# Holding back the second layer's first weight loads until the gathers of expert rows have landed

## What is computed

```python
c_act = jax.nn.silu(c)
for l in range(DEPTH):
    mod = jnp.einsum('bd,dn->bn', c_act, w_ada[l]) + b_ada[l]
    sh1, sc1, gt1, sh2, sc2, gt2 = jnp.split(mod[:, None, :], 6, axis=-1)
    h = rmsnorm(x, g_norm1[l]) * (1.0 + sc1) + sh1
    x = x + gt1 * hybrid_mixer(h, w_in[l], ...)
    h = rmsnorm(x, g_norm2[l]) * (1.0 + sc2) + sh2
    x = x + gt2 * grouped_moe(h, w_router, b_router, w_gate[l], w_up[l], w_down[l])
return rmsnorm(x, g_final)
```

## Time and profile before

| | us |
|---|---|
| median of three runs | 1037.66 |
| lowest, highest | 1033.07, 1038.24 |
| the profiled execution's own time | 1034.82 |
| its span in the profile | 1033.0 |
| PE busy in the span | 980.5 |
| DVE busy | 585.8 |
| ACT busy | 313.7 |
| POOL busy | 88.2 |

### The profile page before, as it was taken

The page is one execution under the profiler, slowest core; times in us unless marked ns, Lnnn a source line. Parts: engine busy times, 40 slices in busy tenths (PEclk is TensorE's granted clock), DMA queues, the critical chain, the costliest instruction groups (busy, mean ns, idle before and its releaser), DMA issues.

```text
span 1033.0 us, 13163 instructions
## 1 busy us (share of the span) xinstructions
PE 980.5 (95%) x4871; PEld 613.3 (59%) x4871; DVE 585.8 (57%) x1350; ACT 313.7 (30%) x781; POOL 88.2 (9%) x83
## 2 busy tenths in 40 slices
PE   3899999999999899999989999999999998999996
PEld 1344465689745557666654445568885556577672
DVE  1359897867656643223185689796763346322327
ACT  3131323656421221112142122436662121211213
POOL 3001003000000010000140010300000000100012
PEclk9899999999999999999989999999999998999998
DMA  9986526600375699999937371140006128999946
GB/s 355 366 278 239 183 72 215 245 2 1 124 279 149 260 338 406 420 418 358 317 128 293 143 265 62 44 163 2 1 2 244 41 111 340 403 410 419 417 145 239
DMA packets 86183, 229.72 MB, mean 222 GB/s; under 512 B 35796, under 2 KB 50628, under 8 KB 71628
## 3 DMA queue, kind: packets, MB, share of 16 engines
q1 hardware_dynamic: 77192, 196.38, 50.6%
q0 software_dynamic: 5760, 20.97, 5.6%
q10 hardware_dynamic: 3168, 11.54, 2.7%
HBM read 210.99 MB, written 22.56 MB: 226 GB/s over the span
## 4 chain that ended last, share of the span: by engine, by line
PE 88%; DVE 4%; DMA 3%; ACT 2%; issue 1%; SPq 1%; POOL 0%; DVEq 0%; ACTq 0%; POOLq 0%
PE bank L1274 80%; PE bank L1291 5%; PE bank L1582 2%; DMA wbuf<-in_w_ada 2%; ACT shared L554 1%; DMA y_rows<-tok 1%; DVE x L1227 1%; DMA shared<-y_rows,ints 1%; SPq L1773 1%; DVE x L1236 0%; POOL shared L518 0%; DVE tok L1000 0%; ACT L644 0%; PE bank L1623 0%; DVE pring L1243 0%
## 5 line engine op out<-in xcount | busy, mean ns | idle before, releaser
L1274 PE MATMUL bank<-shared,wbuf 128*128 128x512 f32 (+2 forms) x640 | 240.4, 534 | 0.8 <-ACT shared L554 0.8
L1274 PE MATMUL bank<-shared 128*128 128x128 f32 (+4 forms) x1248 | 215.8, 329 | 1.8 <-DVE modT L804 1.8
L1274 PE MATMUL bank<-wbuf,shared 128*128 128x512 f32 (+3 forms) x672 | 198.4, 494 | 1.4 <-ACT shared L554 1.4
L1274 PEld LDWEIGHTS bank<-shared,wbuf 128*128 128x128 f32 (+1 forms) x640 | 110.5, 190 | 125.7 <-issue 119.7
L1274 PEld LDWEIGHTS bank<-shared 128*128 128x128 f32 (+1 forms) x1248 | 149.1, 188 | 28.5 <-issue 28.5
L1274 PEld LDWEIGHTS bank<-wbuf,shared 128*128 128x128 f32 (+1 forms) x672 | 99.5, 178 | 79.7 <-issue 74.3
L1274 PEld LDWEIGHTS bank<-shared,pring 128*128 128x128 f32 (+1 forms) x640 | 86.9, 187 | 29.4 <-issue 19.0
L1274 PE MATMUL bank<-shared,pring 128*128 128x64 f32 (+1 forms) x640 | 95.3, 290 | 0.0
L554 ACT ACTIVATE shared<-bank 64x512 f32<-64x512 f32 (+3 forms) x86 | 48.7, 569 | 150.1 <-PE bank L1274 131.7
L1166 DVE TENSOR_TENSOR tring<-bank,tring 128x256 f32<-128x256 f32 x22 | 9.3, 425 | 145.2 <-ACT tring L701 145.2
L644 ACT ACTIVATE tring<-tring,small 128x384 f32<-128x384 f32 (+5 forms) x128 | 69.3, 541 | 51.7 <-DVE small L933 49.9
(11 more groups left out here) (241 smaller groups left out, 1019.9 us busy)
## 6 DMA issues: line engine op xcount, KB each, us to landing
wbuf<-in_w_ada SPq DMA_DIRECT2D x36, 1024.0 KB, 6.4
shared<-in_w_gate SPq DMA_DIRECT2D x20, 1024.0 KB, 14.8
shared<-in_w_up SPq DMA_DIRECT2D x20, 1024.0 KB, 17.9
shared<-in_w_down SPq DMA_DIRECT2D x20, 1024.0 KB, 17.3
shared<-in_w_ada SPq DMA_DIRECT2D x12, 1024.0 KB, 10.3
wbuf<-in_w_in SPq DMA_DIRECT2D x8, 1536.0 KB, 6.5
wbuf<-in_w_gate SPq DMA_DIRECT2D x12, 1024.0 KB, 10.9
wbuf<-in_w_up SPq DMA_DIRECT2D x12, 1024.0 KB, 13.1
```

What stands on the lines that cost most here:

```text
L1274: return nc.tensor.matmul(dst, lhsT, rhs, start=first, stop=last)
```

## The change

In the second layer SP waits for all four `choice_landed` semaphores, at the value that they have when the first layer's eight gathers have landed (`l * totals[landed]`, 32 for each), before it issues the three blocks of `w_ada` and chunk 1 of `w_in`. Chunk 0 is issued ahead of the wait, as before. In the first layer the loop is empty. Nothing else changes.

```diff
@@ -1813,6 +1813,8 @@
                     sp.dma_start(ada_slot(b), layer(whose, w_ada).rearrange("a k n -> (a k) n")[k * P:(k + 1) * P, at:at + ADA_SLOT])\
                         .then_inc(ada_landed[SLOT_OF[b]], 16)
 
+                for landed in choice_landed if l else []:
+                    sp.wait_ge(landed, l * totals[landed])
                 for b in range(3):
                     load_ada(b)
                 if l == 0:
```

## The result

Eight runs of each kernel on one chip: the changed kernel takes 1029.20 us (1027.93 to 1032.45), the kernel before 1035.31 us (1033.07 to 1038.24). The ratio is 0.9941, with a 95% interval of 0.9927 to 0.9954: 0.59% faster, some 6 us. The forecast was 1029.5 us and a gain of 6.8 us. The profiled execution took 1028.14 us, 6.68 us less than that of before; the spans differ by 6.7 us.

A forecast was written before the change was run, and what follows sets the result against it. PE bounds the kernel (88% of the chain), waiting between layers for a store and gathers delayed by loads. DVE's 6.8 us, smaller than PE's 7.2, with late loads free, taken from 1036.2 gives 1029.5 us; range 1025.5 to 1036.5.

The forecast's parts named there:

- The store: End of layer 1: last store lands in 2.6 us instead of 8.44, first gather at 504.5 instead of 510.33.
- DVE's sums: End of layer 1: start at 512.3, sixth ends at 522.6, last near 524.8 instead of 531.60; gain 6.8 us.
- PE's last matmuls: Last 12 of layer 1: 5.31 us instead of 8.11, ending at 523.7, 7.2 us earlier, ahead of DVE's last sum.
- What moves along: Token tile 2's diagonal matrix, 1.94 us, moves with the last sum; stall unchanged, PE gets on at 526.8.
- The loads, late: Held-back 4.7 MB issued by 522, landed between 531 and 535; costs nothing, 17 us to spare on PE.
- my estimate of 27.7 us: Held-back loads one after another at 6.15 us per MB: chunk 1 lands at about 549, third block at 540.
- My slack for DVE: Start of layer 2: DVE needs its first `w_ada` block at 531.7, landed by 526; 5 us to spare.
- Rival A: Store held up by more than the blocks, even share of engines about 5.2 us; gain 4.4, 1031.8 us; chance 0.16.
- Rival B: Gain reaches layer 2 but a later wait takes it, or spread hides it; gain 0 to 4, near 1034; chance 0.11.
- Rival C: Held-back loads too late for PE, chunk 1 after 559.1 us; layer 8 us slower, 1044.5 us; chance 0.04.
- The sum: 6.8 us gained at the start of layer 2 and held to the end; from 1036.2, forecast 1029.5 us; chance 0.68.

The follow-up runs named there:

- e2: Against the kernel before: only chunk 1 waits for the gathers, the three blocks of `w_ada` go out early as before; ratio 1.0001.
- e3: Against the kernel before: chunk 1 issued right behind chunk 0, only the three blocks of `w_ada` wait for the gathers; ratio 0.9954.
- e8: Against the kernel before: nothing held back, but chunk 1 issued ahead of the three blocks of `w_ada`; one run, 1035.87 us.
- e9: Against the kernel before: two blocks of `w_ada` go out early, the third and chunk 1 wait for the gathers; one run, 1034.59 us.
- e4: Against the kernel before: four extra matmuls on PE where it stood idle for layer 1's gathers, to keep its clock up; ratio 0.9993.
- e1: Against the changed kernel: SP's loads wait only for the last store's landing, not for the gathers; ratio to the kernel before 1.0020.
- e12: Against the kernel before: SP's loads wait for a POOL signal placed behind its last gather, which came before the fourth gather started; ratio 1.0015.
- e10: The changed kernel run once more, against the same runs of the kernel before; ratio 0.9929.
- e6: Against the kernel before: the three blocks and chunk 1 wait until PE has finished layer 2's first product; ratio 0.9974.
- e11: Against the kernel before: chunk 0 also waits for the gathers to land, with the other loads behind it; ratio 0.9946.
- e5: Against the kernel before: the three blocks and chunk 1 wait for layer 1's last diagonal matrix; one run, 1029.88 us.

## Why the prediction was right, and where not

**The mechanism** is the one forecast: loads that nobody needs yet held up a store, and behind it eight gathers that PE waits for. e2, e3, e8 and e9 show that the store's lateness goes with what SP has issued ahead of it, e4 that the gain is not mainly the clock (1.2 to 1.8 us of 6.5), e1 and e12 that the gathers must be kept clear as well as the store.

**The store**: 2.6 us forecast, 2.64 measured, first gather at 504.5 forecast and 504.43 measured.

**DVE's sums**: forecast to start at 512.3 and the sixth sum to end at 522.6; the timeline has 512.22 and 522.49 (521.20 + 1.29). The last sum ended at 524.97, forecast 524.8.

**PE's last matmuls**: this step was mis-sized. I had the twelve end at 523.7 and DVE's chain as the later of the two. I gave the last gather the median of six, 6.4 us. It took 7.38 us, PE waited 0.39 us for it and ended at 524.25, and the last sum waited for PE. The stage became 6.5 us shorter, not 6.8. e10 has the same (7.22 us).

**What moves along**: the 1.95 us of the diagonal matrix, unchanged, as forecast.

**The loads, late**: issued by 522.6 (forecast 522), landed by 534.4 (forecast 531 to 535), no wait of PE or DVE for the first three blocks or chunk 1. From 520.58 to there the four took 13.8 us. The rule of the Trainium skill (DMA: Bandwidth & Descriptors, Rules for kernel authors), to issue a DMA early, does not hold here, where the early loads meet a transfer that is on the critical path (8.44 us to land against 2.64); my estimate of 27.7 us from its page's 6.15 us for 1 MB was not seen, since the loads overlap. My slack for DVE, "5 us", was too narrow a reading: e6 was 12 us late for DVE and lost 1.4.

**Rival A** (half the gain) stood on an even share of the engines. The store landed in 2.64 us with chunk 0's tail in front of it, so chunk 0 had no part, and e11 without chunk 0 shows the same. The even share itself was half right, and my argument against it (8.44 is more than twice 2.6) proved nothing. The same page (Queues, rings and completion order) has the engines take turns between queues packet by packet, and the trace agrees once the store is under way: 102 packets of the store and 109 of SP's from 505 to 508 us, though with SP's packets twice as large. Ahead of that lies a stretch that I had not seen, in which the store moved nothing (501 to 504.6 us); whether its packets stood in their queue by then, no run shows.

**Rival B** (given back later): no; the rest of the span is 494.6 and 494.5 us in these two profiles. Single profiles of the rest spread over 3 us, so it is the ratios of the whole time, 0.9941 and in e10 0.9929, that bear this out. **Rival C** (too late): shown by e6 to begin between 8 and 19 us behind the point chosen (e5 and e6, measured from the store's issue), and to be mild there. (By its own terms, 1036.2 + 8, its time would have been 1044.2 us, not 1044.5.)

**The sum**: 6.8 forecast, 6.7 between the two profiles, 6.1 between the medians. That 1029.5 came within 0.3 us of 1029.20 is partly luck: the base that I took, 1036.2, was 0.9 us above the median of the eight runs, and the gain 0.7 us above the medians' difference, and the two cancel.

## What to carry to other kernels

Before a chain of small transfers that the critical engine waits for, look at what else stands in the load queues: in this kernel 4.7 MB of prefetch, issued 2 to 4 us ahead of the first of them, cost 6.5 us, and 4.7 MB issued in the middle of the gathers cost up to 9.7 us (e12 against the changed kernel). A prefetch that has 17 us to spare should wait for the landing of the urgent transfers, not for their issue. And price a late transfer with the clock: in e9 PE's longer wait made the matmuls that followed 2.7 us slower, of which 1.9 reached the stage.

## What the runs showed of the hardware that was not expected

- The store's delay by loads of another queue stopped growing: 5.01, 6.85 and 8.91 us with 1.57, 2.10 and 3.15 MB in front, 8.4 to 8.7 with 4.72. In the kernel before the store's packets do not start for 3.7 us, with SP's queue full; behind that the queues alternate packet for packet (102 and 109), though the one's are 4 KB and the other's 8.
- Gathers lose more when loads come in while they are under way than when the loads had been queued first: medians for those into `shared` of 6.2 us (before) against 14.1 (e1) and 13.9 (e12). In the kernel before, SP's last load had landed by 513.1 us, behind the issue of the third gather, so most gathers had the engines to themselves; in e1 they alternate with SP's packets (468 and 467 from 522 to 528 us).
- A semaphore increment behind a gather in POOL's program took effect (508.34, SP's load at 508.39) while five gathers ahead of it had not yet started (508.56 to 513.53, e12).
